# A new order of loads, additions and finals at the end, and more constant products and a split gather in the routing

## The reference, cut to what matters

```python
def hier_moe(x, p):
    xf = x.reshape(bt * t, dm)
    g_logits = xf @ p['router_g'] + p['router_g_b']
    g_idx = argmax(g_logits)
    ...
    top_v, top_i = lax.top_k(e_in, MOE_TOPK)
    top_w = softmax(top_v) * g_w
    hid = silu(einsum('nd,edf->nef', xf, p['w_gate'])) * einsum('nd,edf->nef', xf, p['w_up'])
    y = einsum('nef,efd->nd', hid * gates[..., None], p['w_down'])

yp = yp + hier_moe(rmsnorm(yp, norm_ffn[layer]), mp)
y_prompt = rmsnorm(yp, norm_final)
```

## Time and profile before

| what | value |
|---|---|
| median of 3 timed runs | 589.94 us (586.92 to 590.29) |
| the profiled execution's own time | 587.77 us |
| its span in the profile | 585.7 us |
| mean granted TensorE clock | 0.991 |
| busy share of PE, PEld, DVE, ACT, POOL | 96%, 53%, 43%, 26%, 14% |
| memory traffic over the span | 414 GB/s |

### The profile page before, as it was taken

One profiled execution on the slowest core, in us unless ns is written; L12 is line 12 of the kernel. 1 busy time (PEld: TensorE's weight loads), 2 busy tenths in 40 slices (PEclk: granted clock), 3 DMA queues, 4 the chain that ended last, 5 costly groups with the idle time before them and its releaser, 6 DMA issues. The chain is left out here.

```text
span 585.7 us, 8561 instructions
## 1 busy us (share of the span) xinstructions
PE 563.7 (96%) x3450; PEld 312.8 (53%) x3450; DVE 249.4 (43%) x595; ACT 154.5 (26%) x327; POOL 79.3 (14%) x116
## 2 busy tenths in 40 slices
PE   6999999999899999999999999999999899999994
PEld 5677877543633333336977555667654543333331
DVE  6999683224741211145542615260113652221147
ACT  6142185221301011024245103254104300101113
POOL 5960700000111210000100001000000021120000
PEclk9899999999999999999999999999999999999998
DMA  8995999897899999999899997999799999999972
GB/s 336 415 346 61 214 408 384 361 397 333 327 374 412 419 421 420 376 331 398 353 426 320 416 397 281 323 338 422 308 374 418 385 376 412 421 421 419 386 249 92
DMA packets 39930, 208.95 MB, mean 357 GB/s; under 512 B 12819, under 2 KB 14547, under 8 KB 23920
## 3 DMA queue, kind: packets, MB, share of 16 engines
q1 hardware_dynamic: 30416, 169.93, 74.8%
q0 software_dynamic: 7872, 34.53, 16.2%
q10 hardware_dynamic: 1600, 3.90, 1.7%
HBM read 198.77 MB, written 43.74 MB: 414 GB/s over the span
## 5 line engine op out<-in xcount | busy, mean ns | idle before, releaser
L1503 PE MATMUL bank<-arena 128*64 128x512 f32 x264 | 87.0, 611 | 0.2 <-DVE arena L1843 0.2
L1503 PE MATMUL bank<-ring,arena 128*64 128x512 f32 x232 | 74.4, 598 | 0.2 <-DVE arena L1843 0.2
L2318 PE MATMUL bank<-arena,ring 128*128 128x320 f32 x256 | 71.6, 434 | 0.0
L2318 PEld LDWEIGHTS bank<-arena,ring 128*128 128x128 f32 x256 | 48.0, 190 | 21.3 <-issue 1.6
L1503 PEld LDWEIGHTS bank<-arena 128*64 128x64 f32 x264 | 24.4, 140 | 32.8 <-issue 32.7
L577 PE MATMUL bank<-xnT,ring 128*128 128x320 f32 x144 | 41.1, 448 | 0.5 <-DVE xnT L896 0.5
L1424 PE MATMUL bank<-ring,arena 128*128 128x512 f32 x92 | 40.3, 594 | 1.0 <-PEq L455 0.6
L1534 PE MATMUL bank<-arena 128*64 128x512 f32 x136 | 39.8, 594 | 0.7 <-ACT arena L1757 0.7
L1977 DVE COPY arena<-bank 128x512 f32<-128x512 f32 x14 | 9.7, 691 | 68.3 <-PE bank L1534 68.3
L1534 PE MATMUL bank<-ring,arena 128*64 128x512 f32 x120 | 36.1, 593 | 0.7 <-ACT arena L1757 0.7
L577 PEld LDWEIGHTS bank<-xnT,ring 128*128 128x128 f32 x144 | 28.0, 196 | 12.4 <-issue 1.2
(11 more groups left out here) (450 smaller groups left out, 853.7 us busy)
## 6 DMA issues: line engine op xcount, KB each, us to landing
arena<-in_w_moe SPq DMA_DIRECT2D x50, 1024.0 KB, 16.1
ring<-in_w_moe SPq DMA_DIRECT2D x44, 1024.0 KB, 15.0
arena<-in_stream_b SPq DMA_DIRECT2D x4, 2560.0 KB, 15.0
out_o_d_old<-in_cache_d_g POOLq DMA_DIRECT2D x1, 8448.0 KB, 29.8
arena<-in_stream_a SPq DMA_DIRECT2D x4, 2048.0 KB, 10.6
out_o_d_old<-in_cache_d_g POOLq DMA_DIRECT2D x1, 7680.0 KB, 40.4
out_o_d_old<-in_cache_d_g SPq DMA_DIRECT2D x1, 4608.0 KB, 37.9
ring<-in_w_out_even SPq DMA_DIRECT2D x2, 2048.0 KB, 11.7
```

The costliest lines, as they stand in the source:

```text
L1503: last = nc.tensor.matmul(c.bank[2 + j % 2][half, :], xgT[:, j % 2, q, half], w[i][q // 4][:, q % 4, :], start=(q == 0), stop=(q == KC - 1))
L2318: last = nc.tensor.matmul(bank(name)[:, 0:TOK], w[:, k, i * P:(i + 1) * P], xnT[:, k, :], start=(k == 0), stop=(k == KC - 1))
```

## The change

In the routing of both layers, `keep_clock_up` is called once more, ahead of the waits for `tri_ok` and `sel_ok` of the first two tiles: 2 products in layer 0, 5 in layer 1. The call ahead of the wait for `sel_ok` of the third tile goes from 2 to 4 products. `gather_first(1)` is split: its first four column blocks stay where it was, the other four go behind the counting products `places((2,))`.

At the end of layer 1 SyncE loads the sample rows first, then t = 0, then t = 1 in two halves with a semaphore each (the second takes over the place of `diag_ok`, which layer 1 doesn't use). VectorE adds them in the same order, 2, 0, 1, and waits for the second half of t = 1 only ahead of its second addition. The final of t = 0 moves ahead of the additions of `add_rows` for t = 1. Layer 0's end keeps its order.

```diff
+EARLIER_ORDER = ((0, 1, 2), (2, 0, 1))
-    diag_ok, summed, cnt_ok, g_in, rows_final = s("diag"), s("summed"), s("overflow_count"), s("final_gain"), s("final_out")
+    diag_ok = yp_hi = s(("diag", "rows_in1_hi")[layer])
+    summed, cnt_ok, g_in, rows_final = s("summed"), s("overflow_count"), s("final_gain"), s("final_out")
-                    for t in range(3):
-                        sp.dma_start(m["yp"][t][0:ROWS[t]], rows[t * P:t * P + ROWS[t], :]).then_inc(yp_in[t], 16)
+                    for t in EARLIER_ORDER[layer]:
+                        if layer == 1 and t == 1:
+                            for q in range(2):
+                                sp.dma_start(m["yp"][t][:, q * D:(q + 1) * D], rows[t * P:t * P + P, q * D:(q + 1) * D])\
+                                    .then_inc(yp_hi if q else yp_in[t], 16)
+                        else:
+                            sp.dma_start(m["yp"][t][0:ROWS[t]], rows[t * P:t * P + ROWS[t], :]).then_inc(yp_in[t], 16)
...
             project_samples(3, n_parts - 1)
             if layer == 1:
                 project_samples(n_parts - 1, n_parts)
+            c.keep_clock_up(c.bank[0], 2 if layer == 0 else 5, 256)
             pe.wait_ge(tri_ok, 1)
             pe.wait_ge(sel_ok, 1)
...
             logits_back(2)
-            gather_first(1)
-            c.keep_clock_up(c.bank[0], 2, 256)
+            gather_first(1, 0, 4)
+            c.keep_clock_up(c.bank[0], 4, 256)
             pe.wait_ge(sel_ok, 2)
             places((2,))
             for u in range(3):
                 last = nc.tensor.matmul(c.bank[7][:, 64:80], ones, m["sum"][:, u, :], start=(u == 0), stop=(u == 2))
             last.then_inc(pos_pe, 1)
+            gather_first(1, 4, KC)
             pe.wait_ge(S0_ok, 2)
...
             def earlier_rows(t, between=None):
-                dve.wait_ge(yp_in[t], 16)
                 rows = ROWS[t]
                 r = c.resid[0:rows, t]
                 for q in range(2):
+                    dve.wait_ge(yp_hi if layer == 1 and t == 1 and q == 1 else yp_in[t], 16)
...
             else:
+                earlier_rows(2)
+                earlier_rows(0)
                 earlier_rows(1)
-                earlier_rows(2)
                 add_rows(sum_first, 0, 0)
                 add_rows(sum_first + 1, 0, 1)
                 add_rows(sum_first + 2, 2, 0)
                 add_rows(sum_first + 3, 2, 1)
                 next_mean(next_norm, 0)
+                next_rows_of(next_norm, 0, 0)
                 add_rows(sum_first + 5, 1, 0)
                 add_rows(sum_first + 7, 1, 1)
                 next_mean(next_norm, 2)
-                next_rows_of(next_norm, 0, 0)
                 next_rows_of(next_norm, 2, 0)
```

More of the change, by code:

```diff
@@ L2027, in earlier_rows @@
                 ins.then_inc(earlier_ok, 1)
-                dve.wait_ge(earlier_ok, t + 1)
+                dve.wait_ge(earlier_ok, EARLIER_ORDER[layer].index(t) + 1)
             hidden(0)
@@ L2086, in next_rows_of @@
                     v.tensor_scalar(next_rows[1], c.resid[:, 1], c.stat[:, 13:14], None, ALU.mult).then_inc(sems["rows1"], 1)
-            earlier_rows(0)
             if layer == 0:
+                earlier_rows(0)
                 earlier_rows(1)
```

## The result

The changed kernel takes 590.9 us in the median (587.89 to 594.18 in 20 executions); the kernel before, on the same chip, 588.52 us (585.61 to 591.63, 20 executions). The ratio is 1.0049 [1.0032, 1.0066], some 2.9 us slower: small, but outside what the measurement leaves open, and on the other side of the forecast of 587.5 us. The profiled execution took 589.52 us with a span of 587.4 us and a mean granted clock of 0.994, against 587.77, 585.7 and 0.991 before.

What follows compares the result with a forecast made beforehand. TensorE was taken to bound the kernel until the weights come late, VectorE the end. Layer 0 -1.2, layer 1 +0.6 and the end -0.6 gave -1.2 us against a mean of 588.7: 587.5 us, range 584.6 to 590.2.

Steps and rivals of the forecast that it cites:

- Layer 0's -1.2 us: Layer 0's routing and first pair: 1.57 us won by holding the clock, less a 0.35 us later start.
- the end's -0.6 us: End of layer 1: the last store goes out at 581.25 instead of 581.88 us; bounds 0 and -0.9.
- The constant products' price: Routing, on TensorE: each constant product costs 0.43 us, taken from two products in 1.03 us.
- Layer 0's overrun: Layer 0's routing: products outlast idle time by 0.15 us (at most 0.3); first pair 0.35 late (0.2 to 0.6).
- -1.57 us: Layer 0's first pair: the clock stays at 2.4 GHz, so its gate and up product saves 1.57 us.
- I count the gain as kept: After layer 0's first pair: gathered rows and weights don't take back the gain, despite a 1.2 us margin at pair 7.
- The rival with the weights: Pair 7's weights use up the 1.2 us margin; layer 0 gives 0.3 us, sum -0.3, 588.4 us; chance 0.10.
- +0.6: Layer 1's routing: five products overrun their gap, so `turn(1)` comes 0.6 us later; bounds +0.2 and +0.9.
- The bytes are the same and the last of them landed at 571.0 so far, so every load just makes it: Layer 1's end: reordered loads land in time for VectorE, so the earlier rows' additions end 1.1 us earlier, at 572.6.
- their bytes explain: Layer 1's end: landings 3 to 4 us apart for 0.5 to 1 MB come from bytes, not a serial 2 us cost.
- The added final in front costs 0.2: Layer 1's end: with t = 0's final moved ahead, t = 1's second addition ends at 578.2, against 578.0.
- the constant products overrun and decide: Rival at layer 1's first `sel_ok` wait: overruns at upper bounds, no clock or end gain; +1.5 us, 590.2; chance 0.13.

Runs made afterwards that it cites:

- e1: The change's routing part alone, in both layers, added to the kernel before; the end as before: 590.31 us, ratio 1.0033 [1.0003, 1.0063].
- e3: The kernel before with only the final of t = 0 moved ahead of the additions for t = 1: 587.19 us, ratio 0.9979 [0.9952, 1.0007].
- e5: The routing part in layer 0 alone, added to the kernel before: 589.97 us, ratio 1.0036 [1.0006, 1.0066].
- e6: The routing part in layer 1 alone (five constant products, the split), added to the kernel before: 589.15 us, ratio 1.0031 [1.0007, 1.0054].
- e7: e6 with 15 constant products in place of 5 ahead of layer 1's first wait: 593.81 us, ratio 1.0093 [1.0059, 1.0127] to the kernel before.
- e2: The change's end part alone, added to the kernel before; the routing as before: 588.84 us, ratio 0.9985 [0.9959, 1.0011].
- e4: The end part alone with t = 1 in one load, order 2, 0, 1 kept: 588.48 us, ratio 0.9995 [0.9963, 1.0027] to the kernel before.
- e8: End part, sample rows' load as one of 128 partitions x 4 KB, their sums wrong: 585.91 us, ratio 0.9968 [0.9947, 0.9989] to the kernel before.
- e9: The kernel before with layer 1's three tiles each loaded in two halves, order 0, 1, 2: 588.02 us, ratio 0.9995 [0.9975, 1.0015].
- e13: End part, old routing; sample rows in two 64 x 4 KB loads on two queues, ScalarE copying second choices down: 588.57 us, 1.0011 to the kernel before.
- e18: e8 with its load as two of 64 x 4 KB, sums still wrong: 587.96 us, ratio 0.9992 [0.9963, 1.0021] to the kernel before.
- e16: e13 with one transfer in place of two for both runs of 64 rows: 597.22 us, ratio 1.0151 [1.0113, 1.0189] to the kernel before.
- e11: The kernel before with only two constant products added ahead of layer 1's first wait: 588.47 us, ratio 1.0008 [0.9988, 1.0028].
- e12: End part's order, old routing and finals; sample rows' load in two on two queues, VectorE adding second choices: 589.36 us, 1.0026 to the kernel before.
- e14: e13 with the routing part, two constant products ahead of the first wait in both layers: 591.81 us, ratio 1.0057 [1.0032, 1.0083] to the kernel before.
- e15: e13 with the final of t = 0 at its old place: 588.60 us, ratio 1.0006 [0.9983, 1.0029] to the kernel before.

## Why the prediction was wrong

Two terms of the sum failed. Layer 0's -1.2 us counted a clock's gain as kept that the next stages took back, and the end's -0.6 us counted on loads that came late. By its ratio the routing part alone (forecast -0.6) measured +1.9 us [0.2 to 3.7], the end part alone -0.9 us [-2.4 to +0.6], so the times blame the first; how the 2.9 us of the whole divide stays open.

*The constant products' price* was right, 0.43 us. *Layer 0's overrun* came to its sum, 0.35 us, by luck: I had 0.15 ahead of `places`, at most 0.3, and the rest behind it; the rows show 0.34 and 0.01. In layer 1 it is the same, 1.02 ahead of `places` for a forecast of 0.75, and -0.15 behind it. Full price beyond the idle time would be 0.30 and 0.98. So the products don't begin early enough to save anything, and the second half of `gather_first(1)` costs nothing.

*"-1.57 us" for the clock, and "I count the gain as kept"*: right for the profiled execution, -1.58, and wrong as a term of the median. The fall was in half of the old routing's profiles, so it could be worth an estimated 0.8 us at most; and the profiles without it were 1.2 us longer up to layer 1's projection, not shorter. The rival with the weights named the right kind of bound and one of its places: pair 7's piece at 241 us was late in three profiles, by up to 2.15 us; more often it is the rows of `y_rows` some 20 us further on, which the prediction doesn't name. Timed alone, layer 0's part costs 2.1 us by its ratio [0.4 to 3.9], of which the rows show the 0.34. How often the exchange happens in timed executions can't be read, so the rest stays open.

*"+0.6" for layer 1's routing*: +0.61 in the pair of profiles, but 0.26 of what was given back was that one execution's: in 16 of the 19 other profiles `up` to `turn` takes 7.01 to 7.03 us, with no wait for the gather. Against those the part costs 1.02 - 0.15 = 0.87 us, my upper bound.

*"The bytes are the same and the last of them landed at 571.0 so far, so every load just makes it"* is the step that failed at the end. I had the row that speaks against it: 13.2 us for 512 KB beside 8.6 us for 1024 KB, and put it down to its place in the queue. That landings 3 to 4 us apart for 0.5 to 1 MB are what "their bytes explain" was misread as well: the 1 MB of t = 1 landed 4.1 us behind t = 0, and the sample rows' 0.5 MB still took 3.2 us. The load was slow by its shape, and put first it held back what stood behind it. In profiles without a fall ahead of the end the additions take 10.5 to 11.7 us with the old order (e1, e3, e5, e6, e7; 9.73 in the kernel before) and 11.6 to 13.0 with the new (the changed kernel, e2, e4), where I had -1.1. With e8's load the rest of the step is right: the last store 17.40 us behind last up against 581.88 - 563.94 = 17.94 before, -0.54 for a forecast of -0.6. *"The added final in front costs 0.2"* assumed that as well; with late additions it costs 0.5.

Of the end's loss the timed runs of e2 show nothing, 0.9985 [0.9959, 1.0011]. The profiled execution before had additions of 9.73 us, among the best of the old order, so the +3.56 of the pair of profiles is more than a typical pair would show. What the ratios give is: routing alone 1.0033, end alone 0.9985, both 1.0049. The routing's and that of both lie in each other's intervals, the end's in neither. The slower side is carried by the routing part, as far as the times show it; that the end adds to it when both stand together is argued from the profiles, not shown by the times.

*The rivals*: "the constant products overrun and decide", which I gave 0.13 and 590.2 us, named the side and most of the size, with the clock "wasn't down in the timed runs" and the upper half of t = 1 late. Its place, layer 1's first wait, gives only 0.87 us of it.

No kernel here that computes the whole is shown to beat the kernel before. e8's load order would be worth 0.5 us by the profile and 1.9 us by its ratio, but it needs the sample rows' second choices stored 64 rows behind their first ones, which means other scatter indices and wasn't tried.

## What to carry to other kernels

Before a load is moved ahead of others, compare its time for its bytes with its neighbours': one that was slow at the end of a queue can be slow by its shape, and at the front it slows everything; look for a window with a full DMA share and half of the traffic. A fall of the clock that one profile shows is no term of a median until several profiles have it, and time won ahead of a stage is only exchanged when that stage waits for a transfer that, though issued earlier, lands no earlier. Filler ahead of a wait is free up to the idle time and costs its full price beyond.

## What the runs showed of the hardware that was not expected

- 512 KB to 64 partitions, in 8 KB or 4 KB rows, in one transfer or in two, held the whole traffic at 166 to 258 GB/s with the DMA engines' share near 1 (the changed kernel, e9, e13, e18); as one transfer over 128 partitions the traffic was 324 to 412 (e8).
- Two such loads on two queues, to both halves of the partitions at the same time, were slow as well: 10.0 us from issue to landing in e13, where e8's one load took 7.0.
- One transfer written as two runs of 64 rows took 17.5 us to land (e16), and held two of the 16 landings of each load behind it; the same bytes in one run took 7.0 us (e8).
- The clock's fall moves: at 158 us in 8 of 20 profiles, at 264 to 272 us in e3, e11, e12, e14 and e15, between 470 and 477 us in e11, e12 and e15 (at 463 too in e15), and a kernel's profiles don't say where its next execution has it. Over all timed executions the mean granted clock was 0.992 before and 0.991 after, so more constant products didn't raise it.
